# 19 of the 1024 tile dots: multiplied by GpSimd, summed by ScalarE

## The chip, the cores and the metric

The kernel runs on one core of one Trainium2 chip. The metric is the device time of one execution in microseconds (us), lower is better. The core has TensorE (PE in the profile; PEld is its weight load), VectorE (DVE), ScalarE (ACT), GpSimd (POOL) and SyncE (SP), which run their own instruction streams and meet at semaphores.

## What is computed

One inference step of a 2-layer hybrid recurrent decoder trunk, for 512 prompt tokens and 8 sample tokens, all in fp32. Layer 0 has a gated DeltaNet and a Mamba-2 mixer side by side, layer 1 a gated linear attention. Behind each mixer comes a retrieval over 16384 single-neuron experts, in which the change lies:

```python
def peer_ffn(h, w_q, keys1, keys2, u_tab, v_tab):
    def block(tb):
        q = (tb @ w_q).reshape(blk, PEER_HEADS, 2, half)
        ...
        v1, i1 = lax.top_k(s1, PEER_TOPK)
        v2, i2 = lax.top_k(s2, PEER_TOPK)
        cand = v1[..., :, None] + v2[..., None, :]
        ...
        top_s, top_j = lax.top_k(cand, PEER_TOPK)
        gate = jax.nn.softmax(top_s, axis=-1)
        pre = jnp.einsum('thkd,td->thk', u_tab[expert], tb)
        act = jax.nn.gelu(pre) * gate
        return jnp.einsum('thk,thkd->td', act, v_tab[expert])
```

Each token has 8 heads with 16 experts each, 128 picks. A pick reads one row of u (1024 numbers), which is multiplied with the token's vector and summed (the dot), and one row of v, which is weighed by gelu(dot) times the gate and added up.

## The kernel before

**Tiles and picks.** The prompt tokens make four tiles of 128, the sample tokens a fifth of 8. The kernel walks through `UNITS`, layer 0 tiles 0 to 3 and then layer 1 tiles 0 to 3, and in each unit through its 128 picks (8 sample picks are mixed into tile 3 of each layer): 1040 picks, numbered g from 0. For one pick, one gather brings the row [u, v] of 2048 numbers for each of 128 partitions, 1 MB, into slot g mod 8 of `ring`. Each half tile of 64 tokens is spread over the 128 partitions, so that picks 0 to 63 of a tile are its first half (w = 0) and picks 64 to 127 its second.

**One pick on each engine.** The order is fixed by hand, the same loop over g on every engine:
- GpSimd waits until `v_done` says that PE is done with pick g - 8, then issues the gather of g (L596).
- DVE waits for the gather and does the dot in one instruction, a product of `ring` and `htok` with a summed output into `pre` (L2357), and counts `dotted`.
- ACT waits for `dotted`, then runs three short operations: gelu into `act_v`, times the gate into `gated`, and a 128x64 scaled mask into `diag` (all recorded under the helper's line L1206).
- PE waits for `diag` and multiplies it with the v half of the ring slot (`tile_v`, two 128x512 products of a 64-column weight, recorded in four matmuls under the helper's line L613), and counts `v_done`.

**The work beside it.** Everything else of the model (projections, scans, norms, top-k choices of the next tiles) is written as generators, `front`, `choose` and `fold`, whose steps have slot numbers: behind pick g each engine runs all steps with a slot up to g. PE takes them two picks ahead (`LEAD`). So during picks 0 to 127 of tile 0 the second half of the even mixer runs: its input projection (two slots for a block of 8 matmuls), the copies of that projection out of PSUM on ACT, the convolution on DVE (L1637), the top-k choice for tile 1 on DVE (L2151 to L2179, with products over 128x2048 at L2100, L2104 and L2118, sums at L2106 and L2120, and the copies to `picked` and `gates` at L2126), and later the scan, with products on GpSimd too (L524). ACT has a table load (`ACT_TABLE_LOAD`) each time it goes from one kind of function to another that isn't in the loaded set.

**Queues.** Every engine works in order. GpSimd's queue holds the gathers, single DMAs for states and convolution rows, eight products of 264 columns (L507) and the products of the scan (L524). Weights are loaded by SP into `wring`.

## Time and profile before

| | us |
|---|---|
| median of 3 runs | 3359.38 (3356.14 to 3359.39) |
| the profiled execution | 3360.97, its span 3359.0 |
| busy PE, DVE, POOL, ACT | 2711.8, 2104.4, 1241.5, 1231.8 |
| 1024 tile dots on DVE (L2357) | 1243.2, 1227 ns each |
| mean granted TensorE clock | 0.84 |
| DMA moved | 1225.88 MB, mean 365 GB/s |

The page cuts the span into 40 slices of 84 us. In the slices from 588 us on, the DMA engines are busy for nine tenths nearly everywhere; in the fourth to seventh, from 252 to 588 us, it is 4, 6, 9 and 8 tenths, with 176 to 403 GB/s. How to read the views: the table of windows gives for each stretch of the span what each engine was busy, in us, and the TensorE clock granted; the rows in order of time give the start, the duration, the engine, the line, and in brackets the idle time before the instruction and what released it; the list of waits adds up such idle times by who waited for whom. Busy times of one engine can overlap a little, since an instruction may start while the one before it is draining.

### The profile page before, as it was taken

The numbers are of one execution on the slowest core, as the hardware profiler recorded it, in microseconds if no ns is written. First come the engines' busy times: TensorE is split into PE (matmuls) and PEld (weight loads), VectorE is DVE, ScalarE is ACT, GpSimd is POOL, SyncE is SP. The second block draws the span as 40 slices with busy tenths as digits, with TensorE's granted clock in tenths as the row PEclk, the third lists the DMA queues.
The fourth block names the chain that finished last, engine by engine and source line by source line (L and its number), as shares of the span: only waits on it lengthen the run. The fifth ranks groups of instructions, "written<-read, shape, count | busy, mean of one in ns | idle before, by whom it ended". The sixth has DMA issues, their size and how long they took to land.

```text
span 3359.0 us, 34624 instructions
## 1 busy us (share of the span) xinstructions
PE 2711.8 (81%) x11134; PEld 1371.6 (41%) x11134; DVE 2104.4 (63%) x4889; ACT 1231.8 (37%) x3752; POOL 1241.5 (37%) x1101
## 2 busy tenths in 40 slices
PE   8879997888988689788976789788789666676776
PEld 7767653444544145344522345344344111111132
DVE  4454688775656787576466785566546776744554
ACT  3211365442333343443333343532333343333332
POOL 0100133663433433344343433344333443433442
PEclk9889997996899789799988799797789776766677
DMA  4204698999999999999999999999899999999997
GB/s 158 76 1 176 246 403 329 389 395 375 408 408 395 401 419 395 388 388 387 418 421 421 405 419 409 368 390 413 368 412 372 400 419 421 397 422 422 421 419 327
DMA packets 186152, 1225.88 MB, mean 365 GB/s; under 512 B 21297, under 2 KB 24129, under 8 KB 50802
## 3 DMA queue, kind: packets, MB, share of 16 engines
q0 software_dynamic: 153024, 1115.00, 81.8%
q1 hardware_dynamic: 32946, 108.67, 8.6%
q8 instruction: 88, 1.44, 0.2%
q14 instruction: 94, 0.77, 0.1%
HBM read 1211.74 MB, written 11.84 MB: 364 GB/s over the span
## 4 chain that ended last, share of the span: by engine, by line
PE 48%; DMA 26%; DVE 15%; ACT 5%; issue 3%; DVEq 2%; POOL 1%; SPq 0%; ACTq 0%; POOLq 0%
PE ps L613 47%; DMA ring<-in_uv,picked 24%; DVE ring L2357 6%; DVEq L2149 1%; ACT scratch L1206 1%; ACT diag L1206 1%; ACT L1206 1%; DVE scratch L2100 1%; ACT gated L1206 1%; DMA scratch<-in_keys 1%; POOL ring L596 1%; ACT act_v L1206 1%; DVE scratch L2118 0%; DVE scratch L2104 0%; DVE ids L2106 0%
## 5 line engine op out<-in xcount | busy, mean ns | idle before, releaser
L596 POOL DMA_INDIRECT ring<-in_uv,picked x1024 | 1166.3, 1139 | 1744.6 <-PE ps L613 1635.3
L613 PE MATMUL ps<-ring,diag 128*64 128x512 f32 x4096 | 1339.8, 749 | 481.6 <-ACT diag L1206 474.7
L2357 DVE SCALAR_TENSOR_TENSOR ring<-ring,htok 128x1024 f32<-128x1024 f32 x1024 | 1243.2, 1227 | 596.0 <-DMA ring<-in_uv,picked 590.8
L613 PE MATMUL ps<-hT,wring 128*128 128x256 f32 (+1 forms) x3200 | 802.1, 401 | 18.4 <-DVE hT L1600 8.7
L1206 ACT ACTIVATE act_v<-pre 128x1 f32<-128x1 f32 x1040 | 209.5, 201 | 1467.3 <-DVE ring L2357 1466.3
L613 PEld LDWEIGHTS ps<-hT,wring 128*128 128x128 f32 x3200 | 602.6, 195 | 326.2 <-issue 229.8
L613 PEld LDWEIGHTS ps<-ring,diag 128*64 128x64 f32 x4096 | 245.1, 156 | 1188.4 <-ACT diag L1206 997.6
L1206 ACT ACTIVATE diag<-folded,gated 128x64 f32<-128x64 f32 x1024 | 356.2, 348 | 36.0 <-PE ps L613 2.7
L1206 ACT ACTIVATE gated<-act_v,gates 128x1 f32<-128x1 f32 x1024 | 301.7, 295 | 33.3
L613 PEld LDWEIGHTS ps<-scratch 128*128 128x128 f32 (+2 forms) x1428 | 201.5, 209 | 147.6 <-issue 85.5
L613 PE MATMUL ps<-scratch 128*128 128x128 f32 (+5 forms) x1428 | 238.0, 312 | 28.4 <-DVE scratch L1747 15.1
L1206 ACT ACTIVATE scratch<-ps 128x256 f32<-128x256 f32 (+5 forms) x118 | 64.7, 548 | 207.7 <-PE ps L613 206.9
L1206 ACT ACT_TABLE_LOAD x97 | 124.5, 1283 | 2.4 <-PEq L2463 0.7
L1206 ACT ACTIVATE keep<-ps 128x264 f32<-128x264 f32 (+4 forms) x147 | 43.6, 327 | 139.6 <-PE ps L613 139.5
L1637 DVE SCALAR_TENSOR_TENSOR keep<-keep,conv_w 128x256 f32<-128x256 f32 x120 | 58.1, 484 | 51.7 <-ACT keep L1206 43.1
L2357 DVE DVE_READ_ACCUMULATOR ring<-ring,htok 128x1 f32 x1024 | 83.5, 82 | 0.0
L524 POOL TENSOR_TENSOR scratch<-scratch,masks 128x512 f32<-128x512 f32 x18 | 25.9, 1447 | 152.1 <-DVE scratch L1724 141.0
L2306 DVE TENSOR_TENSOR xT<-xT,ps 128x512 f32<-128x512 f32 x15 | 10.3, 687 | 96.4 <-PE ps L1075 96.4
L2151 DVE MAX8 scratch<-scratch 128x8 f32<-128x128 f32 (+1 forms) x168 | 35.4, 259 | 56.1 <-ACT scratch L1206 55.4
L613 PE MATMUL ps<-gated,ring 128*128 128x1 f32 x256 | 42.6, 296 | 16.4 <-ACT gated L1206 16.4
L1620 DVE TENSOR_TENSOR xT<-ps,xT 128x256 f32<-128x256 f32 (+1 forms) x32 | 13.7, 428 | 64.9 <-PE ps L613 64.9
L613 PEld LDWEIGHTS ps<-gated,ring 128*128 128x128 f32 x256 | 41.3, 253 | 30.5 <-ACT gated L1206 30.5
(340 smaller groups left out, 1734.3 us busy)
## 6 DMA issues: line engine op xcount, KB each, us to landing
wring<-in_weights SPq DMA_DIRECT2D x200, 512.0 KB, 7.8
ring<-in_uv,picked POOLq DMA_INDIRECT x1024, 13.3
scratch<-in_keys POOLq DMA_DIRECT2D x4, 1024.0 KB, 14.6
scratch<-in_s_gla POOLq DMA_DIRECT2D x4, 1024.0 KB, 12.7
out_o_gla<-scratch POOLq DMA_DIRECT2D x4, 1024.0 KB, 12.8
scratch<-in_s_dn POOLq DMA_DIRECT2D x1, 2048.0 KB, 14.4
scratch<-in_s_ssm POOLq DMA_DIRECT2D x1, 2048.0 KB, 19.9
out_o_dn<-scratch POOLq DMA_DIRECT2D x1, 2048.0 KB, 11.8
```

The source lines that it names most:

```text
L524: pool.tensor_tensor(nl[:, (6 * m + l - 1) % 4, :].rearrange("p (h i) -> p h i", h=4), nmat, mask4(LEVEL0 + l), ALU.mult).then_inc(sem(f"n ...
L596: pool.indirect_dma_start(out=ring[:, g % RING, :], out_offset=None, in_=io["uv"][L], in_offset=bass.IndirectOffsetOnAxis(ap=index, axis=0 ...
L613: return pe.matmul(out, lhsT, rhs, start=start, stop=stop)
L1206: return act.activation(out, in_, func, **k)
L1620: tt(x, ps[:, 2 + b % 2, 0:n], x, ADD).then_inc(sem("gemm_free"), 1)
L1637: last = stt(y, x[:, 3 - s:259 - s], conv_w[:, j, 3 - s:4 - s], y, MUL, ADD)
L2100: tt(e, posf[R, H].rearrange("p h (k a) -> p (h k) a", a=1).to_broadcast(full), each(iota[:, :] if step == 8 else row_at).to_broadcast(ful ...
L2149: dve.drain()
L2151: dve.max(vals[:, 0:8], src)
L2306: last = tt(x, x, ps[:, w % 2, :].rearrange("p (c h i) -> p h c i", c=4, h=2), ADD)
L2357: stt(x, x, 1.0, h, MUL, MUL, accum_out=pre[:, g % SMALL:g % SMALL + 1]).then_inc(sem("dotted"), 1)
```

## The change

For picks 8, 11, ..., 62 of the first unit (`BY_POOL`, 19 picks) the dot is split. GpSimd multiplies the u half of the ring slot with `htok` in place, and ACT sums the product by a copy onto itself with an accumulated output into `pre`, in front of its three short operations. The instruction on DVE goes, and `dots(g)` turns a pick number into the number of dots that DVE has done by then. GpSimd's product for pick m stands in its queue right behind the gather of pick m + 5 (`MULTIPLY_LAG`). Besides, some semaphores are merged (`sample_ready` for three, `htok_mm` takes over `last_rows_mm`), with the same waits. The core of the diff:

```diff
+MULTIPLY_LAG = 5
+BY_POOL = list(range(8, HALF, 3))
+
+
+def dots(g):
+    return g - sum(m < g for m in BY_POOL)
...
@@ gpsimd, behind the gather of pick g @@
+                    m = g - MULTIPLY_LAG
+                    if m in BY_POOL:
+                        pool.wait_ge(sem(f"uv_loaded{m % RING}"), 16 * (m // RING + 1))
+                        pool.wait_ge(sem("fold_ready"), 1)
+                        pool.tensor_tensor(ring[:, m % RING, 0:D], ring[:, m % RING, 0:D], htok[:, 1, :], ALU.mult)\
+                            .then_inc(sem("multiplied"), 1)
                     front.upto(g)
...
@@ scalar, at pick g @@
-                    act.wait_ge(sem("dotted"), g + 1)
+                    if g in BY_POOL:
+                        n = BY_POOL.index(g) + 1
+                        act.wait_ge(sem("multiplied"), n)
+                        x = ring[:, g % RING, 0:D]
+                        f(x, x, ACT.Copy, accum_out=pre[:, s:s + 1]).then_inc(sem("summed"), 1)
+                        act.wait_ge(sem("summed"), n)
+                    else:
+                        act.wait_ge(sem("dotted"), dots(g + 1))
                     f(act_v[:, s:s + 1], pre[:, s:s + 1], ACT.Gelu_apprx_tanh).then_inc(sem("gelu_done"), 1)
...
@@ vector, at pick g @@
-                    dve.wait_ge(sem(f"uv_loaded{g % RING}"), 16 * (g // RING + 1))
                     x = ring[:, g % RING, 0:D]
                     if t == S:
                         x = x.rearrange("p (b i) -> p b i", b=2)
-                    stt(x, x, 1.0, h, MUL, MUL, accum_out=pre[:, g % SMALL:g % SMALL + 1]).then_inc(sem("dotted"), 1)
+                    if g not in BY_POOL:
+                        dve.wait_ge(sem(f"uv_loaded{g % RING}"), 16 * (g // RING + 1))
+                        stt(x, x, 1.0, h, MUL, MUL, accum_out=pre[:, g % SMALL:g % SMALL + 1]).then_inc(sem("dotted"), 1)
```

How the queues read at three places of the changed picks. First GpSimd from gather 41 on, before (gathers are the DMAs into `ring`):

```order
L596 DMA ring<-in_uv,picked 128x2048 x12
L514 DMA out_o_conv_s<-scratch 128x480
L515 DMA out_o_conv_p<-keep 128x60
L596 DMA ring<-in_uv,picked 128x2048 x14
L524 TENSOR_TENSOR scratch<-scratch,masks 128x512
```

and the same place now, from the product for pick 44 on:

```order
L611 TENSOR_TENSOR ring<-ring,htok 128x1024
L604 DMA ring<-in_uv,picked 128x2048 x3
L611 TENSOR_TENSOR ring<-ring,htok 128x1024
L522 DMA out_o_conv_s<-scratch 128x480
L523 DMA out_o_conv_p<-keep 128x60
L604 DMA ring<-in_uv,picked 128x2048 x3
L611 TENSOR_TENSOR ring<-ring,htok 128x1024
L604 DMA ring<-in_uv,picked 128x2048 x3
L611 TENSOR_TENSOR ring<-ring,htok 128x1024
```

The third product there is that for pick 50, behind gather 55; those for picks 53, 56 and 59 follow in the same rhythm, and that for pick 62 stands between the first two products of the scan (L532, before L524).

DVE in the choice for tile 1, before, from the dot of pick 47 to the dot of pick 49:

```order
L2357 SCALAR_TENSOR_TENSOR ring,pre<-ring,htok 128x1024
L2106 TENSOR_REDUCE ids<-scratch 128x128
L2108 CAST scratch<-ids 128x128
L2110 TENSOR_SCALAR scratch<-scratch 128x128
L2357 SCALAR_TENSOR_TENSOR ring,pre<-ring,htok 128x1024
L2112 CAST scratch<-scratch 128x128
L2115 SCALAR_TENSOR_TENSOR ids<-scratch,ids 128x128
L2116 TENSOR_TENSOR scratch<-scratch 128x128
L2100 TENSOR_TENSOR scratch<-scratch,pack 128x2048
L2357 SCALAR_TENSOR_TENSOR ring,pre<-ring,htok 128x1024
```

and now, with the product in front of it:

```order
L2125 TENSOR_TENSOR scratch<-scratch 128x2048
L2127 TENSOR_REDUCE ids<-scratch 128x128
L2129 CAST scratch<-ids 128x128
L2131 TENSOR_SCALAR scratch<-scratch 128x128
L2379 SCALAR_TENSOR_TENSOR ring,pre<-ring,htok 128x1024
L2133 CAST scratch<-scratch 128x128
L2136 SCALAR_TENSOR_TENSOR ids<-scratch,ids 128x128
L2137 TENSOR_TENSOR scratch<-scratch 128x128
L2121 TENSOR_TENSOR scratch<-scratch,pack 128x2048
L2379 SCALAR_TENSOR_TENSOR ring,pre<-ring,htok 128x1024
```

The dot between the second product over 2048 elements and its sum is gone.

ACT at picks 22 and 23, behind a table load; before there are six short operations between two table loads' groups, now a sum over 1024 columns stands in their middle:

```order
L1220 ACT_TABLE_LOAD
L1220 ACTIVATE act_v<-pre 128x1
L1220 ACTIVATE gated<-act_v,gates 128x1
L1220 ACTIVATE diag<-folded,gated 128x64
L1220 ACTIVATE ring,pre<-ring 128x1024
L1220 ACTIVATE act_v<-pre 128x1
L1220 ACTIVATE gated<-act_v,gates 128x1
L1220 ACTIVATE diag<-folded,gated 128x64
```

Only the row `ring,pre<-ring` is new there.

## Rows read from the trace of the kernel before

**Rows 1.** The chain that ended last, shares of the span by engine.
```profile
PE 48%; DMA 26%; DVE 15%; ACT 5%; issue 3%; DVEq 2%; POOL 1%; SPq 0%; ACTq 0%; POOLq 0%
```

**Rows 2.** Windows: stretch, length, busy us of each engine, PEclk, DMA, GB/s.
```profile
480.00:500.00 20.00, 20.00 (x84) 10.12 (x83) 18.50 (x58) 14.37 (x34) 5.82 (x7) 1.00 1.02 415
...
540.00:560.00 20.00, 10.77 (x48) 4.38 (x48) 19.13 (x20) 7.84 (x18) 6.12 (x5) 0.62 0.87 321
```

**Rows 3.** Waits from 400 to 528 us: total us, times, longest.
```profile
POOL ring L596 <- PE ps L613: 87.0, 39, 5.7
```

**Rows 4.** DVE in order of time: start, us, what; idle before in brackets.
```profile
567.84 0.19 DVE L1659 RECIPROCAL keep<-keep 8x8 f32<-8x8 f32 x1 [1.50 <-ACT keep L1206]
...
576.24 1.76 DVE L1715 TENSOR_TENSOR scratch<-scratch,masks 128x1536 f32<-128x1536 f32 x1 [1.25 <-ACT scratch L1206]
```

**Rows 5.** GpSimd and DVE in order of time, where both work.
```profile
354.44 5.66 POOL L507 TENSOR_TENSOR hT<-hT,otok 128x264 f32<-128x264 f32 x8 [22.58 <-ACT hT L1206]
...
592.12 1.21 DVE L2357 SCALAR_TENSOR_TENSOR ring<-ring,htok 128x1024 f32<-128x1024 f32 x1
593.03 1.43 POOL L524 TENSOR_TENSOR scratch<-scratch,masks 128x512 f32<-128x512 f32 x1
593.27 2.27 DVE L2357 SCALAR_TENSOR_TENSOR ring<-ring,htok 128x1024 f32<-128x1024 f32 x1
...
604.96 1.28 POOL L524 TENSOR_TENSOR scratch<-scratch,masks 128x512 f32<-128x512 f32 x1
605.44 0.68 DVE L1747 TENSOR_TENSOR scratch<-scratch,ps 128x512 f32<-128x512 f32 x1
```

**Rows 6.** The gathers (L596) of 440 to 520 us, issue to landing.
```profile
DMA to landing us min/median/max: 7.7/10.1/12.0
```

**Rows 7.** GpSimd's gathers 52 to 67 and DVE behind them, in order of time.
```profile
534.28 0.94 POOL L596 DMA_INDIRECT ring<-in_uv,picked  x1 [0.30 <-issue]
535.36 0.33 DVE L1648 TENSOR_TENSOR scratch<-scratch,conv_w 128x160 f32<-128x160 f32 x1
...
548.65 1.42 POOL L596 DMA_INDIRECT ring<-in_uv,picked  x1 [2.64 <-PE ps L613]
550.24 2.29 DVE L2100 TENSOR_TENSOR scratch<-scratch,pack 128x2048 f32<-128x2048 f32 x1
...
562.28 0.93 POOL L596 DMA_INDIRECT ring<-in_uv,picked  x1 [5.07 <-PE ps L613]
562.99 0.85 DVE L2126 COPY gates<-ids 64x64 f32<-64x64 f32 x4
...
572.29 0.96 DVE L1711 TENSOR_SCALAR scratch<-scratch 128x1536 f32<-128x1536 f32 x1
...
583.72 1.21 POOL L596 DMA_INDIRECT ring<-in_uv,picked  x1 [2.21 <-PE ps L613]
...
589.52 1.77 POOL L596 DMA_INDIRECT ring<-in_uv,picked  x1 [0.16 <-issue]
```

**Rows 8.** ACT, PE and GpSimd in order of time, around ACT's table loads.
```profile
449.31 1.40 POOL L596 DMA_INDIRECT ring<-in_uv,picked  x1 [2.05 <-PE ps L613]
...
455.55 1.28 ACT L1206 ACT_TABLE_LOAD   x1
...
462.12 0.35 ACT L1206 ACTIVATE diag<-folded,gated 128x64 f32<-128x64 f32 x1
462.88 0.65 PE L613 MATMUL ps<-ring,diag 128*64 128x512 f32 x2
...
465.38 1.06 ACT L1206 ACTIVATE keep<-keep 128x1024 f32<-128x1024 f32 x1
...
468.31 0.35 ACT L1206 ACTIVATE diag<-folded,gated 128x64 f32<-128x64 f32 x1
468.85 0.65 PE L613 MATMUL ps<-ring,diag 128*64 128x512 f32 x2
...
573.28 1.58 ACT L1206 ACTIVATE scratch<-scratch 128x1536 f32<-128x1536 f32 x2 [0.35 <-DVE scratch L1711]
```

More of the change, by code:

```diff
@@ L851, in sample_even @@
                 pe.wait_ge(sem("even_group"), 5)
-                pe.wait_ge(sem("sm_diag_ready"), 1)
+                pe.wait_ge(sem("sample_ready"), 1)
                 mm(ps[:, 4, 0:192], ones[0:NS_TOK, :], sm_diag[0:NS_TOK, :, :].rearrange("p b c -> p (b c)"))\
@@ L877, in sample_even @@
                 last.then_inc(sem("sm_o_mm"), 1)
-                pe.wait_ge(sem("sm_xd_ready"), 1)
+                pe.wait_ge(sem("sample_ready"), 2)
                 for b in range(NS_TOK):
@@ L997, in sample_odd @@
                 pe.wait_ge(sem("odd_group"), 5)
-                pe.wait_ge(sem("sm_q_ready"), 1)
+                pe.wait_ge(sem("sample_ready"), 3)
                 for q in range(4):
@@ L1069, in last_rows @@
                                       xT[:, 4 * h + c, TILE_AT[3] + HALF:TILE_AT[3] + P], ident)
-                    last.then_inc(sem("last_rows_mm"), 1)
+                    last.then_inc(sem("htok_mm"), 1)
             def turn(w):
@@ L1110, in choice @@
                     if t == 1 and L:
-                        pe.wait_ge(sem("dotted"), SAMPLE_G[0][-1] + 1)
+                        pe.wait_ge(sem("dotted"), dots(SAMPLE_G[0][-1] + 1))
                     if t == S:
@@ L1149, in spread @@
                 if b >= 2:
-                    pe.wait_ge(sem("dotted"), SAMPLE_G[L][b - 2] + 1)
+                    pe.wait_ge(sem("dotted"), dots(SAMPLE_G[L][b - 2] + 1))
                 for c in range(KD):
@@ L1200, in _ @@
                 last = mm(ps[HALF * s:HALF * s + HALF, 4, 0:1], folded[:, :], row_sum[:, 0:1])
-            last.then_inc(sem("last_rows_mm"), 1)
+            last.then_inc(sem("htok_mm"), 1)
         @block.scalar
@@ L1483, in choice @@
                             for v in BEFORE[SAMPLE[L]]:
-                                act.wait_ge(sem("dotted"), v)
+                                act.wait_ge(sem("dotted"), dots(v))
                             last = f(h_s[:, :, :], hT[:, :, 256:264], ACT.Copy)
@@ L1498, in folds @@
                         act.wait_ge(sem("fold_mm"), 2 * w - 1 + h)
-                        act.wait_ge(sem("dotted"), SUB_FIRST[w - 1])
+                        act.wait_ge(sem("dotted"), dots(SUB_FIRST[w - 1]))
                         f(htok[:, 1 + w % 2, 512 * h:512 * h + 512], ps[:, w % 2, :], ACT.Copy).then_inc(sem("fold_ready"), 1)
@@ L1532, in _ @@
                     if g == ROWS_AT + 2:
-                        act.wait_ge(sem("last_rows_mm"), 1)
+                        act.wait_ge(sem("htok_mm"), max(ROW_TILE) + 1)
                         f(last_y, ps[:, 4, :], ACT.Copy).then_inc(sem("last_rows"), 1)
@@ L1539, in _ @@
             f(s_root, ps[:, 3, 0:NS_TOK], ACT.Sqrt, scale=1.0 / D, bias=eps[:, 0:1]).then_inc(sem("root_ready"), 1)
-            act.wait_ge(sem("last_rows_mm"), 2)
+            act.wait_ge(sem("htok_mm"), max(ROW_TILE) + 2)
             f(row_sum[:, 2:3], ps[:, 4, 0:1], ACT.Sqrt, scale=1.0 / D, bias=eps[:, 0:1]).then_inc(sem("root_ready"), 1)
@@ L1797, in sample_even @@
                    ident[0:NS_TOK, 0:NS_TOK].rearrange("p (b a) -> p b a", a=1).to_broadcast([NS_TOK, NS_TOK, 24]), MUL)\
-                    .then_inc(sem("sm_diag_ready"), 1)
+                    .then_inc(sem("sample_ready"), 1)
                 yield slot(2)
@@ L1805, in sample_even @@
                     last = tt(sm_xd[r], conv[r, 12:16, S_], sm_bc[r, :, 16 + half:24:2].rearrange("p b k -> p k b"), MUL)
-                last.then_inc(sem("sm_xd_ready"), 1)
+                last.then_inc(sem("sample_ready"), 1)
                 yield slot(6)
@@ L2003, in sample_odd @@
                 yield slot(0)
-                tsc(sm_q, oproj[:, 0:4, 256:264], scale, None, MUL).then_inc(sem("sm_q_ready"), 1)
+                tsc(sm_q, oproj[:, 0:4, 256:264], scale, None, MUL).then_inc(sem("sample_ready"), 1)
                 dve.wait_ge(sem("sm_exp"), 2)
```

## The prediction, made before the result

> **What bounds the kernel now.** I read the chain that ended last first, then the stretch in which the changed picks run, in three views: the table of 20 us windows, the list of waits from 400 to 528 us, and the rows of each engine in order of time. The whole span is a stream of 1040 picks in a fixed order, of which each takes one slot of an 8-deep ring, so time lost or won at one pick moves all later picks. The chain names PE for 48%, the gather for 26% and DVE for 15% [rows 1]. The 19 dots that the change takes off DVE are picks 8, 11, ..., 62; they run between 407 us (dot 8) and 591 us (dot 62) of 3359 us. What a dot is worth is decided there and nowhere else.
>
> That stretch has two parts. From pick 8 to about pick 44 (407 to 528 us) **PE leads**: it is busy for 20.00 of 20 us at 480 to 500 while DVE has 1.5 us free and ACT 5.6 [rows 2]. GpSimd's gathers wait for PE, 87.0 us in 39 waits, and it starts one gather per 2.99 us, the time of one pick on PE [rows 3]. From about pick 45 to pick 63 (528 to 592 us) **DVE leads**: 19.13 of 20 us busy at 540 to 560 while PE has 10.77 us and its granted clock is 0.62 [rows 2]; PE now waits for ACT's diag, and ACT for the dot.
>
> **What the change removes.** A dot costs 1.22 us, and the next instruction of DVE starts 1.14 to 1.15 us after it (dot 63 at 592.12, dot 64 at 593.27) [rows 5]. In the part that PE leads, 13 dots (8 to 44) leave: worth nothing there, since their diag is ready before PE takes it. In the part that DVE leads, six leave (47, 50, 53, 56, 59, 62), 6 x 1.14 = 6.8 us at most. Two of them are not on DVE's path: after dots 52 and 53 DVE sits 1.50 us until ACT has written what it inverts at 567.84, and after the place of dot 56 it sits 1.25 us until ACT releases the product at 576.24 [rows 4]. So 4 x 1.14 = **-4.6 us**.
>
> **What it adds on GpSimd.** A two-input product of 264 columns took 5.66 / 8 = 0.71 us there and one of 512 columns 1.28 us [rows 5]. That is (1.28 - 0.71) / 248 = 2.3 ns a column, so 1024 columns take 1.28 + 512 x 0.0023 = **2.5 us**. Such a product shuts out DVE. Dot 64 starts at 593.27, as dot 63 ends and while GpSimd is in its product of 593.03 to 594.46, and takes 2.27 us instead of 1.21: the 1.19 us that the two overlap, nearly all of it [rows 5]. Not everything is shut out: a sum whose second input is in PSUM took 0.68 us beside a GpSimd product at 604.96 [rows 5]. So an instruction of DVE with both inputs in SBUF waits until GpSimd has ended, and one with an input in PSUM doesn't; I take one with a single input to go free too. The Trainium skill ("SBUF — State Buffer", Who interferes with whom) states this as an exclusive lock on a shared pair of ports that the first to start holds for its whole instruction; by that rule, the rows agree, and it speaks against this change. It adds that copies of fp32 between SBUF tensors in DVE's two-port mode are shut out as well, which bears on one row of rows 7 (the copies of gates) and on nothing else in the sum. The skill's "GPSIMD Engine Reference" (Elementwise — side-by-side cycle accounting) gives 4497 ns for 2048 columns; by half of it, an estimate of 2.25 us, the next sum would be about 1 us smaller.
>
> Where each of the six products lands follows from the program's order: the product for pick m is queued on GpSimd right behind gather m + 5, which waits until PE is done with pick m - 3. Gathers landed 10.1 us after issue in the middle and 12.0 us at most [rows 6], and gather m is then five picks old, about 15 us, so the product waits for no data. What DVE loses, from [rows 7], where the gathers 52, 55, 58, 61, 64 and 67 are the GpSimd rows:
> - pick 47: free from 534.28 + 0.94 = 535.22, ends 537.7. DVE is in a run of two-input products of 160 columns; the next, at 535.36, waits: 2.3 us.
> - pick 50: free from 550.07, ends 552.6; the product of 2048 columns at 550.24 waits: 2.3 us.
> - pick 53: free from 563.21, ends 565.7; the copies of gates and dot 52 wait: 2.4 us.
> - pick 56: free from about 572.4, when DVE's one input operation of 1536 columns has started at 572.29; it ends before DVE's next two-input work at 576.24: 0.
> - pick 59: free from 584.93, ends 587.4; DVE has two sums with an input in PSUM until about 585.9 and then dot 60: 1.5 us.
> - pick 62: free from 591.3, just behind the start of dot 63, then dot 64 waits 2.5 us where it waited 1.06 already, and GpSimd's own product for the scan comes later: 1.9 us, my value between 1.4 and 2.5.
> The sum is **+10.4 us**. The bounds are 0 (all six beside work with one input) and 6 x 2.5 = 15 us. I take the value near the upper end because three quarters of DVE's time in this part is in instructions with two inputs in SBUF or in copies.
>
> **What it adds on ACT.** A pass over 128x1024 in SBUF took 1.06 us at 465.38 [rows 8]; the summing copy is priced by it, no row shows the accumulation itself, so 1.0 to 1.4 us. ACT has 14.37 of 20 us busy at 480 to 500 us [rows 2], so 19 x 1.06 = 20 us mostly lies beside other work. Two places have no room. One is pick 53, whose sum stands before ACT's work for the scan at 573.28: 1.06 less the 0.35 us that ACT sat there [rows 8], **+0.7 us**. The other is picks 20 to 24, around ACT's table loads. Gather 25 is issued at 449.31 and ends at 450.7, the product for pick 20 ends at 453.2, its sum at 454.3, its three short operations at 455.2, those of pick 21 at 457.1 (its dot, behind a convolution that waits for an ACT copy held up by pick 17's sum, is ready about 456.2) and the copies of the projection at 458.1, where the first table load began at 455.55: 2.5 us late. Then comes pick 22, whose diag started at 462.12 and ended at 462.47 when PE took it at 462.88 (0.4 us of slack), the sum for pick 23 (1.06 us more) and pick 24, whose diag ended at 468.66 for a PE that took it at 468.85 (0.2 us) [rows 8]. 2.5 + 1.1 - 0.2 = **+3.4 us**, and PE leads there, so the end pays it. Bounds: 0, if the product is early, and 5 us.
>
> In the rest of the part that PE leads, diag is 2 to 7 us ahead of PE, and a product costs this lead 2 to 4 us for the moment; I put it at 0.
>
> **Sum.** -4.6 + 10.4 + 0.7 + 3.4 = +9.9 us. The profiled execution took 3360.97 us (span 3359.0), so it would take 3370.9 us; it was 1.6 us above the median of 3359.38 us, so the median becomes **3369.3 us**. What a measurement of this kernel tells from no change is 0.2%, 6.7 us.
>
> **The rivals.**
> - *The port is cheap* (faster). If GpSimd gets its turn only when DVE is in an instruction with one input or waits for ACT, DVE loses nothing and keeps the relief of all six: 3359.4 - 6.8 = 3352.6 us. It decides below 1.14 us lost per product. For it: DVE has reduces of 2.29 us and sums from PSUM, and the 56 case. Against it: in [rows 5] GpSimd's product of 593.03 gets its turn as dot 63 ends, ahead of dot 64. Chance 0.14, of which 0.10 are faster by over 0.2%. The skill's page "Perfetto Trace Analysis" (Optimizing Scalar/DVE Operations) says that moving work off a saturated DVE may make sense and also that between these two engines it might not help; that is this rival and my forecast side by side.
> - *ACT has room*. The table loads hide in PE's lead and only the port is paid: 3359.4 + 6.5 = 3365.9 us. For it: its diag is 2 to 7 us ahead of PE at most picks. Chance 0.20, 0.12 of it within 0.2%.
> - *The product comes too late everywhere*. From PE's end of pick m - 3: gather 1.2, product 2.5, sum 1.1, three short operations 0.95, the copies 1.0, the convolution and top-k on DVE 2.3, dot m + 1 1.15, its three 0.95, which is 11.2 us for a PE that wants it after 10.9. With a port wait, each of 13 products then costs about 1 us: 3369.3 - 3.4 + 13 = 3378.9 us. Chance 0.15.
> - *Given back later*: after 600 us the gathers carry much of the path, and a shift at pick 63 is absorbed, 3359 to 3361 us. Against it: a gather waits for PE's pick eight back, so it moves along. Chance 0.13.
> - *It doesn't do what it says*: excluded, the order has 19 products on GpSimd, 19 sums on ACT and 19 dots fewer on DVE.
>
> **How the numbers follow.** The forecast itself has 0.38, of which 0.02 within 0.2%. Faster: 0.10. Same: 0.04 + 0.12 + 0.13 + 0.02 = 0.31. Slower: 0.36 + 0.08 + 0.15 = 0.59. The likeliest case gives 3369.3 us. Its own unknowns (port 5 to 15 us, ACT 0 to 5 us) make 3361 to 3376; the range reaches over most of the late product and of the absorbed case, 3355 to 3380 us, and leaves out the full relief.
>
> **What would show it.** Right: 19 products on GpSimd of 2.4 to 2.6 us; dots and 2048-column products of DVE with a share of 2 us and more longer than now; PE waiting for ACT's diag at picks 22 and 24; dot 64 starting about 10 us later. Wrong: no DVE instruction grown between 528 and 592 us (port), or pick 63 done no later than now.

## The result, and the profile after

The changed kernel takes **3386.37 us** (median of 4 runs, 3382.02 to 3387.32) where the kernel before took 3357.76 us beside it (4 runs, 3353.45 to 3359.39): a ratio of 1.0077, 95% interval 1.0064 to 1.0090. It is slower, as predicted, but by 28.6 us and not by 10, and that lies outside the range. The profiled execution spans 3385.5 us; the span was 3359.0 before.

The page of the changed kernel: busy time of each engine, the chain that ended last, and two groups of instructions.

```profile
PE 2713.2 (80%) x11134; PEld 1364.4 (40%) x11134; DVE 2125.2 (63%) x4851; ACT 1255.1 (37%) x3790; POOL 1275.2 (38%) x1120
...
PE 43%; DMA 26%; DVE 17%; ACT 7%; issue 3%; DVEq 2%; POOL 1%; another core or an unknown queue 0%; SPq 0%; POOLq 0%; ACTq 0%
...
L1658 DVE SCALAR_TENSOR_TENSOR keep<-keep,conv_w 128x256 f32<-128x256 f32 x120 | 73.9, 616 | 52.1 <-ACT keep L1220 44.1
```

DVE lost 19 dots and is still busy for **longer**: 2125.2 us against 2104.4. The convolution's products, which nobody touched, have a mean of 616 ns, and of 484 ns on the page before:

```profile
L1637 DVE SCALAR_TENSOR_TENSOR keep<-keep,conv_w 128x256 f32<-128x256 f32 x120 | 58.1, 484 | 51.7 <-ACT keep L1206 43.1
```

In the chain PE has gone from 48% to 43%, DVE from 15% to 17% and ACT from 5% to 7% [rows 1].

The windows of [rows 2] in the changed kernel, with the wait of [rows 3] (from 400 to 528 us) under them:

```profile
480.00:500.00 20.00, 20.00 (x83) 10.17 (x84) 18.08 (x51) 10.26 (x29) 10.26 (x8) 1.00 0.99 390
540.00:560.00 20.00, 7.89 (x16) 1.18 (x16) 17.63 (x43) 15.12 (x28) 9.90 (x9) 0.55 0.77 282
...
POOL ring L604 <- PE ps L627: 59.3, 27, 5.9
```

PE still has no free time at 480 to 500 us, but gathers wait for it only 27 times and not 39. At 540 to 560 us PE is down from 10.77 to 7.89 us. The windows are fixed in time: what stands in the second one now ran 10 to 15 us earlier before, so they show how full the engines are and not what one piece of work costs.

Where the time is lost is read from the gathers, since gather g starts when PE is done with pick g - 8. The gathers 10 and 76 of the kernel before:

```profile
400.63 0.94 POOL L596 DMA_INDIRECT ring<-in_uv,picked  x1 [2.94 <-PE ps L613]
...
613.80 1.38 POOL L596 DMA_INDIRECT ring<-in_uv,picked  x1 [1.57 <-PE ps L613]
```

and of the changed kernel:

```profile
398.23 0.94 POOL L604 DMA_INDIRECT ring<-in_uv,picked  x1 [2.93 <-PE ps L627]
...
641.15 1.39 POOL L604 DMA_INDIRECT ring<-in_uv,picked  x1 [1.56 <-PE ps L627]
```

The first is 2.40 us early, ahead of any product, which is only how one execution differs from another. The stretch between the two is 242.92 us long and was 213.17: **29.75 us** more. The span is 26.5 us longer from a start that is 2.4 us early, so 28.9 of it is still there at the end. I call this the shift of a kernel, and read it at two places: at pick 41 (gather 49), about where PE stops leading, and at pick 68 (gather 76). Up to pick 20 it is under 1 us. It grows by 6.7 us at picks 21 to 23, by 3.5 at 32 and 33, by 9.2 at 42 to 45 (2.0 of it gone at pick 46), by 7.7 at 52 to 54 (4.7 of it gone at pick 56), by 5.2 at 57 to 60 and by 3.4 at 61 and 62. A gather can also start late because GpSimd itself is late, so single picks stand out and fall back; what counts is what stays.

The product itself is as predicted, 19 of them at 2.35 to 2.52 us:

```profile
L611 POOL TENSOR_TENSOR ring<-ring,htok x19: 2349/2358/2515, 408.1 to 613.2; 128x1024 f32<-128x1024 f32 x19
```

What it does to DVE, in order of time (start, us, what; one pair around ScalarE's table loads, and three of the DVE-led part):

```profile
457.59 3.59 DVE L2379 SCALAR_TENSOR_TENSOR ring<-ring,htok 128x1024 f32<-128x1024 f32 x1
457.73 2.36 POOL L611 TENSOR_TENSOR ring<-ring,htok 128x1024 f32<-128x1024 f32 x1
...
538.50 2.35 POOL L611 TENSOR_TENSOR ring<-ring,htok 128x1024 f32<-128x1024 f32 x1
538.72 3.21 DVE L2379 SCALAR_TENSOR_TENSOR ring<-ring,htok 128x1024 f32<-128x1024 f32 x1
...
565.45 2.95 DVE L2136 SCALAR_TENSOR_TENSOR ids<-scratch,ids 128x128 f32<-128x128 f32 x1
565.88 2.37 POOL L611 TENSOR_TENSOR ring<-ring,htok 128x1024 f32<-128x1024 f32 x1
...
579.06 2.50 POOL L611 TENSOR_TENSOR ring<-ring,htok 128x1024 f32<-128x1024 f32 x1
579.46 2.76 DVE L2147 CAST picked<-ids 64x64 uint32<-64x64 f32 x4
```

A dot of 1.21 us takes 3.59 us, the whole product more, although its record starts 0.14 us before the product's. An operation of 128 columns takes 2.95 us. The product for pick 44 is the second pair: it stands at 538.50, five gathers behind its own, behind gather 49, which before was issued at 529.83, and so already in the part that DVE leads.

### The profile page after: what moved, and what is told of

Its sections match the earlier page's. It is cut to its first block, busy times and chain, and to the rows that moved or that the text cites. A ratio compares the mean times of both kernels' runs of the same rounds, so it can differ in the third digit from the quotient of the medians.

```text
span 3385.5 us, 34662 instructions
## 1 busy us (share of the span) xinstructions
PE 2713.2 (80%) x11134; PEld 1364.4 (40%) x11134; DVE 2125.2 (63%) x4851; ACT 1255.1 (37%) x3790; POOL 1275.2 (38%) x1120
## 3 DMA queue, kind: packets, MB, share of 16 engines
q8 instruction: 88, 1.44, 0.2%
## 4 chain that ended last, share of the span: by engine, by line
PE 43%; DMA 26%; DVE 17%; ACT 7%; issue 3%; DVEq 2%; POOL 1%; another core or an unknown queue 0%; SPq 0%; POOLq 0%; ACTq 0%
PE ps L627 43%; DMA ring<-in_uv,picked 24%; DVE ring L2379 6%; ACT L1220 1%; DVEq L2170 1%; ACT diag L1220 1%; ACT gated L1220 1%; ACT scratch L1220 1%; POOL ring L604 1%; DMA scratch<-in_keys 1%; DVE scratch L2121 1%; DVE keep L1658 1%; ACT act_v L1220 1%; ACT keep L1220 1%; DVE scratch L2125 0%
## 5 line engine op out<-in xcount | busy, mean ns | idle before, releaser
L604 POOL DMA_INDIRECT ring<-in_uv,picked x1024 | 1154.5, 1127 | 1740.0 <-PE ps L627 1634.6
L1658 DVE SCALAR_TENSOR_TENSOR keep<-keep,conv_w 128x256 f32<-128x256 f32 x120 | 73.9, 616 | 52.1 <-ACT keep L1220 44.1
L532 POOL TENSOR_TENSOR scratch<-scratch,masks 128x512 f32<-128x512 f32 x18 | 24.7, 1381 | 151.7 <-DVE scratch L1745 141.4
L627 PEld LDWEIGHTS ps<-masks,keep 128*128 128x128 f32 x288 | 39.4, 212 | 24.9 <-issue 24.8
## 6 DMA issues: line engine op xcount, KB each, us to landing
scratch<-in_s_gla POOLq DMA_DIRECT2D x4, 1024.0 KB, 12.5
scratch<-in_s_dn POOLq DMA_DIRECT2D x1, 2048.0 KB, 14.9
```

The source lines that it names most:

```text
L532: pool.tensor_tensor(nl[:, (6 * m + l - 1) % 4, :].rearrange("p (h i) -> p h i", h=4), nmat, mask4(LEVEL0 + l), ALU.mult).then_inc(sem(f"n ...
L604: pool.indirect_dma_start(out=ring[:, g % RING, :], out_offset=None, in_=io["uv"][L], in_offset=bass.IndirectOffsetOnAxis(ap=index, axis=0 ...
L627: return pe.matmul(out, lhsT, rhs, start=start, stop=stop)
L1658: last = stt(y, x[:, 3 - s:259 - s], conv_w[:, j, 3 - s:4 - s], y, MUL, ADD)
```

## The experiments

Each kernel's ratio is to the kernel before, run beside it. One execution differs from another by some us, so the ratio says how much and the shift, from one trace, says where; the two agree within 7.4 us (the most is e1, 16.1 us by the shift and 8.7 by the ratio). The two kernels e2 and e3 have a shift of 1.6 us at pick 41 although nothing that slows them lies before it, and e1 and the changed kernel, which run the same up to there, differ by 2.4 us, so that column is good to 2.4 us. The last column is how much longer than before (2104.4 us) DVE was busy.

| kernel | what runs | ratio, 95% interval | shift at pick 41 | at pick 68 | DVE busy |
|---|---|---|---|---|---|
| changed | all | 1.0077, 1.0064 to 1.0090 | 10.1 | 29.8 | +20.8 |
| e1 | picks 8 to 44 only | 1.0026, 1.0014 to 1.0037 | 12.5 | 16.1 | +15.6 |
| e2 | picks 47 to 62 only | 1.0031, 1.0019 to 1.0043 | 1.6 | 14.8 | +1.9 |
| e3 | 19 dots dropped | 0.9983, 0.9971 to 0.9994 | 1.6 | -1.7 | -20.1 |
| e4 | all dots, free product | 1.0071, 1.0044 to 1.0099 | 9.1 | 29.9 | +39.0 |
| e11 | the same, half as long | 1.0033, 1.0017 to 1.0049 | 2.3 | 16.3 | +27.2 |
| e8 | all dots, memset | 1.0045, 1.0030 to 1.0060 | 1.4 | 9.3 | +9.7 |
| e5 | all dots, free sum | 1.0031, 1.0021 to 1.0042 | 2.0 | 7.6 | +1.3 |
| e7 | changed without sums | 1.0076, 1.0056 to 1.0097 | 8.1 | 22.2 | +14.9 |
| e6 | product after 3 gathers | 1.0041, 1.0026 to 1.0057 | 10.1 | 20.1 | +13.5 |
| e12 | e6 without sums | 1.0038, 1.0023 to 1.0053 | 9.2 | 15.8 | +14.8 |
| e15 | e12 without 17, 20, 23, 26 | 1.0019, 1.0008 to 1.0031 | 0.5 | 7.8 | +9.5 |
| e13 | e6, signal after 5 | 1.0043, 1.0025 to 1.0061 | 6.9 | 20.6 | +17.3 |
| e14 | e3, signal after 5 | 0.9986, 0.9975 to 0.9998 | 0.6 | -2.6 | -18.5 |
| e9 | changed without 17, 20, 23 | 1.0060, 1.0042 to 1.0078 | 9.5 | 26.6 | +15.6 |
| e10 | changed without 59, 62 | 1.0057, 1.0040 to 1.0073 | 10.1 | 23.4 | +21.8 |

**The two halves of the picks.**

```diff
-BY_POOL = list(range(8, HALF, 3))
+BY_POOL = list(range(8, 45, 3))       # e1
+BY_POOL = list(range(47, HALF, 3))    # e2
```

> The change for picks 8 to 44 alone (13 products), the stretch where PE led before. In the profile of the changed kernel the gathers are +12 us behind the kernel before at pick 41 to 44, counted from their lead of 2.4 us before the first product. If the two stretches add up, this kernel is 10 to 13 us slower than before. My recorded sum had 3.4 us for it; if the loss here is later hidden under DVE's work from pick 45 on, it is under 5 us.

> The change for picks 47 to 62 alone (6 products), the stretch where DVE led. My recorded sum had +6.5 us. If the stretches add up as the profile of the changed kernel has it, +14 to +18 us. If what was lost there came from engines that were already out of step from the first stretch, under 8 us.

The shifts add up: 16.1 + 14.8 = 30.9 us, against 29.8. The ratios give 0.26% + 0.31% = 0.57% against 0.77%, which their intervals just allow. By the shifts, the 13 picks that I had priced at 3.4 us cost as much as the six that I had priced at 6.5.

**The relief alone.** e3 takes the products and the sums out and lets ACT wait for the gather, so the dots of 19 picks are left out.

```diff
-                        act.wait_ge(sem("multiplied"), n)
-                        x = ring[:, g % RING, 0:D]
-                        f(x, x, ACT.Copy, accum_out=pre[:, s:s + 1]).then_inc(sem("summed"), 1)
-                        act.wait_ge(sem("summed"), n)
+                        act.wait_ge(sem(f"uv_loaded{g % RING}"), 16 * (g // RING + 1))
```

> The 19 dots are left out altogether: no product on GpSimd, no sum on ACT, ACT uses an old number in their place and waits for the gather alone. This is the most that taking them off DVE can give. By my count 6 dots lie in the stretch where DVE leads and 4 of them on its path: 4.6 to 6.8 us faster than before. If DVE's load reaches PE in the first stretch too, more: up to 19 x 1.14 = 22 us.

Nothing is won up to pick 41, 3.3 us from there to pick 68 (1.6 to -1.7). So 19 dots for nothing are worth 0.17%, and the six that count are worth about three. The merged semaphores of the change are in e3 too, and its shift is 0.0 us up to pick 38: they cost nothing.

**The product alone.** In e4 all dots stay on DVE, and GpSimd's product has another output and is waited for by nobody; e11 halves it, and e8 puts a memset of the same length as e11's product in its place.

```diff
+                        pool.tensor_tensor(otok[:, D // 2:D].bitcast(mybir.dt.bfloat16), htok[:, 1, :], htok[:, 1, :], ALU.mult)           # e4
+                        pool.tensor_tensor(otok[:, D // 2:D // 2 + 256].bitcast(mybir.dt.bfloat16), htok[:, 1, 0:512], htok[:, 1, 0:512], ALU.mult)   # e11
+                        pool.memset(otok[:, D // 2:D].bitcast(mybir.dt.bfloat16), 0.0)           # e8
```

> All dots stay on DVE; GpSimd does 19 products of 1024 columns at the same places of its queue, on htok alone, into a buffer that nobody reads. No sum on ACT and nobody waits for the product. Theory port (a product keeps DVE out of its two-input instructions for its whole length): 19 x 2.4 us of DVE time lost and no dot saved, so at least as slow as the changed kernel, 28 to 40 us slower than before. Theory queue (the time is lost because ACT waits in order for product and sum): under 12 us slower.

> As the kernel with the product alone, but GpSimd fills the unused buffer with zeros instead of multiplying (it writes and reads nothing in SBUF). Shows whether GpSimd's use of SBUF for reads is what keeps DVE out. Theory port, reads: DVE's instructions keep their lengths and the kernel is within 3 us of before. If any GpSimd instruction on SBUF shuts DVE out, it is slower by its own length each time.

> The kernel with all dots on VectorE and a product on GpSimd that nobody waits for, now over 512 columns instead of 1024, some 0.95 us long, as long as the memset of the run before (0.97 us, the kernel 14 us slower by its median, the stage 8.7 us longer). If the port is what costs, VectorE's busy time grows by nearly the whole of each product (19 x 0.9 = 17 us, against 9.7 us with the memset), and the stage by about half of what the full product gave (29 us): 14 to 18 us, the kernel at 3368 to 3375 us. If it is the place in GpSimd's queue that costs, this run gives what the memset gave, a stage 8 to 9 us longer and VectorE's busy time up by 10 us at most.

The lines of GpSimd's operation in e4, e11 and e8 (min, median, max in ns):

```profile
L613 POOL TENSOR_TENSOR otok<-htok x19: 1899/1900/1911, 408.2 to 615.1; 128x1024 bf16<-128x1024 f32 x19
...
L613 POOL TENSOR_TENSOR otok<-htok x19: 1046/1047/1048, 411.6 to 604.8; 128x512 bf16<-128x512 f32 x19
...
L613 POOL MEMSET otok<- x19: 965/965/970, 410.7 to 599.1; 128x1024 bf16 x19
```

e4 has a shift as large as the changed kernel's with no wait for GpSimd in it: ScalarE waits for DVE's dots there and for no product. So the product alone can cost that much. That the two figures are equal is chance, since e4 keeps its 19 dots, has shorter products and no sums. Half the length gives half the shift, 16.3 us. The memset, of nearly the same length and in the same places of the queue, gives 9.3, and DVE is busy for 9.7 us more, where e11 has 27.2. So the inputs that GpSimd reads cost VectorE's time, on top of what a memset does. (The ratios of e8 and e11, 1.0045 and 1.0033, don't tell the two apart; the shift and DVE's busy time do.) A dot and a small copy of DVE in e8, each with its memset:

```profile
420.08 1.21 DVE L2374 SCALAR_TENSOR_TENSOR ring<-ring,htok 128x1024 f32<-128x1024 f32 x1
420.17 0.96 POOL L613 MEMSET otok<- 128x1024 bf16 x1
...
478.51 1.70 DVE L1649 COPY keep<-keep 128x3 f32<-128x3 f32 x1
479.22 0.96 POOL L613 MEMSET otok<- 128x1024 bf16 x1
```

The dot goes on beside the memset in its usual 1.21 us; the copy takes 1.70 us, where such a copy has 0.17. The memset is therefore not free for DVE either. Of the 9.7 us, 8.3 lie in six places, all of them copies, casts or an operation with a constant (TENSOR_SCALAR), each with one input tensor, in SBUF; no dot beside a memset took more than 1.22 us. How much of the 9.3 us of shift is that and how much the gathers behind the memset in the queue stays open. The Trainium skill ("SBUF — State Buffer", Who interferes with whom) has both: a DVE instruction with two SBUF inputs contends with GpSimd instructions that read and not with those that only write, and, without that distinction, copies, casts and the like in the two-port mode contend with GpSimd.

**The sum alone.** e5 adds 19 summing copies to the kernel before, of `htok`, into a spare output; e7 takes them out of the changed kernel (the sums of 19 picks are left out, ACT only waits for the product).

```diff
+                        f(otok[:, D // 2:D].bitcast(mybir.dt.bfloat16), htok[:, 1, :], ACT.Copy, accum_out=spare_sum[:, 0:1]).then_inc(sem("summed"), 1)   # e5
...
-                        f(x, x, ACT.Copy, accum_out=pre[:, s:s + 1]).then_inc(sem("summed"), 1)   # e7
```

> All dots stay on DVE, nothing on GpSimd; ACT does 19 summing copies over 1024 columns (of htok, their result unused) in front of its three short operations at the same picks. It prices ACT's part by itself. My recorded sum had 1.06 us each, of which 0.7 + about 1 us reach the end: 1 to 4 us slower. Theory queue: ACT's load is what counts, 8 us or more.

> The changed kernel without the sum: product on GpSimd and no dot on DVE for the 19 picks, ACT waits for the product but does not sum it (an old number is used). The difference to the changed kernel is the price of the 19 sums in place. Theory port: 1 to 6 us faster than the changed kernel. Theory queue: 8 us or more faster.

Both give 7.6 us of shift, 2.0 of it up to pick 41 (where I had put 3.4) and the rest behind it (0.7). A sum is two instructions, here at pick 62 of the changed kernel:

```profile
615.72 1.06 ACT L1220 ACTIVATE ring<-ring 128x1024 f32<-128x1024 f32 x1 [5.64 <-POOL ring L611]
616.69 0.19 ACT L1220 ACTIVATION_READ_ACCUMULATOR ring<-ring 128x1 f32 x1
```

The ratios of the changed kernel and of e7, though, hardly differ (1.0077 and 1.0076, intervals of 0.2%), so the sum's price is known to some 7 us only.

**Is the product too late?** e6 moves it up to three gathers behind its own, and e12 takes e6's sums out as well (left out for 19 picks).

```diff
-MULTIPLY_LAG = 5
+MULTIPLY_LAG = 3
```

> The changed kernel with the product behind the gather of pick m + 3 instead of m + 5, so some 6 us earlier. Theory queue (ACT waits for a product that comes late): much of the 28 us comes back, the kernel is under 15 us slower than before. Theory port: each product shuts out DVE all the same, 23 us or more slower than before.

> The changed kernel with the product three gathers behind its own instead of five, and without ScalarE's sum (ScalarE only waits for the product; the sums of the 19 picks are left out). With three gathers nobody waited for a product, so this leaves the relief (stage 1.7 us shorter when alone) and what the product does to VectorE. If lateness (about 10 us of stage between five and three gathers) and the sum (about 8 us) add up, the stage is 10 to 14 us longer than before and the kernel at 3363 to 3368 us. If they overlap (the sum costs only because the product is late), it stays near the run with three gathers, 18 to 20 us of stage, 3370 to 3375 us.

In e6 9.7 us of the shift are back, all behind pick 41, and no engine waits for a product any more; the changed kernel had this:

```profile
ACT act_v L1220 <- DVE ring L2379: 74.4, 24, 7.1
ACT ring L1220 <- POOL ring L611: 20.4, 6, 5.6
```

That looks like lateness, and I took it for that. e13 tests it: the products stay where e6 has them, and only ScalarE's signal comes from a one-column memset where the changed kernel's product stood. e14 is e3 with that signal (no products and sums).

```diff
+                    m = g - 5                                             # e13, behind the product of g - 3
+                    if m in BY_POOL:
+                        pool.wait_ge(sem("multiplied"), 2 * BY_POOL.index(m) + 1)
+                        pool.memset(mark[:, 0:1], 0.0).then_inc(sem("multiplied"), 1)
...
-                        act.wait_ge(sem("multiplied"), n)
+                        act.wait_ge(sem("multiplied"), 2 * n)
```

> The kernel with the product three gathers behind its own, but ScalarE waits for a one-column memset of GpSimd that stands where the product stood in the changed kernel, five gathers behind. The products fall where they fall with three gathers (stage 20.1 us longer than before, nobody waits for a product). If lateness makes the 9.7 us between that and the changed kernel (29.8), the stage is 26 to 30 us longer here, the kernel at 3378 to 3386 us. If it is the place of the products, it stays at 19 to 22 us and the kernel at 3366 to 3374 us.

> The 19 dots dropped, no product and no sum, and ScalarE waits at those picks for the row and for a one-column memset that GpSimd does five gathers behind (the products and sums of these 19 picks are left out). If being late costs by itself, the stage is 4 to 9 us longer than before, nearly all of it behind pick 44, the kernel some 3 to 8 us over before. If lateness costs only together with what the products take from VectorE, the stage stays near the run with the dots dropped, 1.7 us shorter than before, within 2 us.

The theory falls. e13 keeps e6's shift (20.6 against 20.1), and e14 is as fast as e3; ScalarE does wait for the mark there, 13.3 us in 7 times, and it costs nothing. So a signal five gathers late is not the price. What differs between e6 and the changed kernel is what the products fall on, and that the product's own 2.4 us come on top of the late place. By the gathers, the changed kernel is behind e6 by 1.9 us at pick 48, 4.4 at 50, 6.5 at 56, 8.9 at 57 and 9.7 at 62. The last of these places can be read, in the next paragraph; what makes the others stays open.

**The end of the stretch.** e10 leaves out the picks 59 and 62 of the changed kernel.

```diff
-BY_POOL = list(range(8, HALF, 3))
+BY_POOL = list(range(8, 57, 3))
```

> The changed kernel without the picks 59 and 62 (17 products). If what the last part costs is that ScalarE waits for products that stand late in GpSimd's queue (5.6 us at pick 62, handed on to VectorE's wait of 10.8 us for TensorE), the stage ends 6 to 9 us earlier than in the changed kernel and the kernel takes 3377 to 3381 us. If VectorE's time lost under the products 47 to 56 makes it (they hold instructions of the top-k choice), under 3 us come back and it stays at 3383 to 3387 us.

6.3 us of the shift are back. Pick 62 in the changed kernel, GpSimd, ACT, PE and DVE in order of time:

```profile
609.97 1.28 POOL scratch L532
611.40 1.77 POOL ring L604
613.19 2.51 POOL ring L611
615.72 1.16 ACT ring L1220 x2
...
617.72 0.58 ACT L1220 ACTIVATE scratch<-ps 128x512 f32<-128x512 f32 x1
618.35 2.08 PE L627 MATMUL ps<-scratch 128*128 128x128 f32 x8 [3.00 <-ACT scratch L1220]
624.30 0.69 DVE L1766 TENSOR_TENSOR scratch<-scratch,ps 128x512 f32<-128x512 f32 x1 [10.81 <-PE ps L627]
```

(The first four lines are from the chain, with their start and time.) The product stands behind gather 67 and GpSimd's own scan product before it. It holds nothing of DVE, which waits for PE by then, so no port is in it. ScalarE waits 5.64 us for the product, and behind the sum in its queue stands the copy that the scan on PE needs; PE waits for that copy, DVE for PE. Here it is the wait for the product.

**ScalarE's table loads.** e9 leaves out the picks 17, 20 and 23 of the changed kernel. e15 leaves 17, 20, 23 and 26 out of e12 (their dots are back on DVE, the other 15 picks stay without a sum).

```diff
+BY_POOL = [m for m in range(8, HALF, 3) if m not in (17, 20, 23)]       # e9
+BY_POOL = [m for m in range(8, HALF, 3) if m not in (17, 20, 23, 26)]   # e15
```

> The changed kernel without the picks 17, 20 and 23 (their dots go back to VectorE, 16 products are left). In the trace of the changed kernel the end of pick 23 on TensorE is 7.5 us later than before, counted from the end of pick 10, and none of it had come by pick 18. If the table loads of ScalarE there (picks 20 to 24) were stretched by its sums, as I predicted, or by products that hold the dots of VectorE, the shift at pick 25 falls to under 2 us and the kernel to 3375 to 3380 us. If VectorE has spare time around there and catches up in either case (rival: the shift is made by other products of the part, and moves to the next table load), the shift comes a few picks later and the kernel stays at 3382 to 3387 us.

> The run with three gathers and no sum, with the dots of picks 17, 20, 23 and 26 back on VectorE (the other 15 picks are still left unsummed). With all 19 products the end of pick 25 on TensorE was 8.6 us late and VectorE had been held by products at 434, 444, 453 and 463 us, ahead of ScalarE's two rows of table loads. If only products ahead of table loads cost in the part that TensorE leads, the shift at pick 40 falls from 9.2 us to under 3 us (1.6 of it stands in runs that change nothing there), and the stage from 15.8 to 8 to 10 us. If the next products do the same to what follows, the shift at pick 40 stays above 5 us.

e9 halves the shift at pick 25 (7.5 to 3.7 us), less than the fall to under 2 us that I had expected. Its trace shows the rest: the product for pick 14, at 433.59, also stands ahead of the table loads. The three convolution products at 432.91 take 4.44 us with it instead of 1.61, the four table loads start 2.5 us late, and PE waits 2.05 us for the diag of pick 22. e15 is clear: at pick 41 the shift is 0.5 us instead of 9.2. Nine other products up to there cost nothing. How four of them cost so much is read in e12, GpSimd and DVE, then ACT and PE in order of time:

```profile
443.51 3.89 DVE L2376 SCALAR_TENSOR_TENSOR ring<-ring,htok 128x1024 f32<-128x1024 f32 x1
443.95 2.36 POOL L611 TENSOR_TENSOR ring<-ring,htok 128x1024 f32<-128x1024 f32 x1
...
453.20 2.36 POOL L611 TENSOR_TENSOR ring<-ring,htok 128x1024 f32<-128x1024 f32 x1
454.15 1.44 DVE L1651 COPY keep<-keep 128x3 f32<-128x3 f32 x1 [0.99 <-ACT keep L1220]
...
458.00 1.22 DVE L2376 SCALAR_TENSOR_TENSOR ring<-ring,htok 128x1024 f32<-128x1024 f32 x1
```

and behind that:

```profile
459.26 0.20 ACT L1220 ACTIVATE act_v<-pre 128x1 f32<-128x1 f32 x1 [4.34 <-DVE ring L2376]
...
460.99 1.28 ACT L1220 ACT_TABLE_LOAD   x1
...
465.70 1.28 ACT L1220 ACT_TABLE_LOAD   x1
...
467.56 0.35 ACT L1220 ACTIVATE diag<-folded,gated 128x64 f32<-128x64 f32 x1
...
467.96 1.98 PE L627 MATMUL ps<-ring,diag 128*64 128x512 f32 x4 [4.68 <-ACT diag L1220]
```

The dot at 458.00, that of pick 21, is itself not held, but it is late: before, it stood at 452.56. Three products in a row, those for picks 17, 20 and 23, have held DVE: the one at 434.50 a dot (3.93 us), the one at 443.95 another (3.89 us), the one at 453.20 a copy of three columns in front of this dot (1.44 us instead of 0.17). ScalarE waits 4.34 us for it, where it waited 2.97 us before:

```profile
453.82 0.20 ACT L1206 ACTIVATE act_v<-pre 128x1 f32<-128x1 f32 x1 [2.97 <-DVE ring L2357]
```

The four table loads stand behind that dot's operations in a fixed order, so they start at 460.99 where they started at 455.55 [rows 8], the next diag comes at 467.56 instead of 462.12, and PE stops for 4.68 us. The lead over PE was enough for the table loads, and not for them and the products ahead of them.

## Why the prediction came out as it did

Right were the direction and the mechanism: GpSimd's product shuts out DVE's instructions with two inputs in SBUF for its whole length (e4: 39.0 us of DVE for 19 products of 1.90 us). So were the product's time (2.5 us predicted, 2.36 measured), the sum's 1.06 us, the products of picks 47 and 50 (2.3 us of DVE each; the instructions at 548.57 and 565.45 took 2.92 and 2.95 us, of which the operation itself is 0.3), pick 56 beside nothing, pick 53 (the casts at 579.46 took 2.76 us instead of 0.80; 2.4 us predicted), and PE waiting for the diag of pick 22 (4.29 us), though not for that of pick 24.

Not right was that an instruction with a single input goes free. It holds for DVE's searches and reduces (in e6 the reduce of 2048 columns at 571.88 keeps its 2.29 us beside the product of 570.25 to 574.03). It doesn't hold for copies and casts, which I had excepted at pick 53, nor for operations with a constant, which I had not. In e4:

```profile
592.10 2.84 DVE L1727 TENSOR_SCALAR scratch<-scratch 128x1536 f32<-128x1536 f32 x1
592.21 1.90 POOL L613 TENSOR_TENSOR otok<-htok 128x1024 bf16<-128x1024 f32 x1
```

That is the instruction of 0.96 us beside which I had put the product for pick 56 at 0. In the changed kernel this product runs from 593.60 to 595.95, while DVE waits for ScalarE; that it cost nothing was luck.

Its size was wrong, and two steps failed, both of them costs that I had put at 0: what the products do to DVE in the part that PE leads, and the place of the products five gathers behind. The terms, with what the shifts give for them:

- **Relief**, -4.6 predicted: -1.7 in all, -3.3 behind pick 41 (e3), which is what three dots are worth and not four.
- **Port**, +10.4: e12 has relief and port alone, 15.8, so the port is 15.8 + 1.7 = **17.5 us**. Behind pick 41 it is 6.6 + 3.3 = 9.9, near my term, though in the places of e12 and not in those that I had worked out. The other 7.6 us are in the part that PE leads, and there I had written "I put it at 0". This is the first step that failed. I had set the lead of 2 to 7 us against one product of 2.4, where several add up, and had looked at the table loads only for ScalarE's sums and the late products (3.4 us) and not for DVE, though my own step noted 0.4 and 0.2 us of slack there. With the sums gone from e12, the jump is all there; with four products gone, none is.
- **Which products lie in which part.** I went by the picks, six of them behind 528 us. The product of pick 44 stands behind gather 49, which was issued at 529.83 before, and so belongs to the part that DVE leads, which I priced without it. e1, which has no later product, still goes from 12.5 to 16.1 us behind pick 41. (The changed kernel grows by 9.2 us between picks 41 and 45, but the product for pick 47 has a share in that.)
- **Single places**: pick 59 held DVE for 0.4 us (1.5 predicted, the dot at 605.82 took 1.57), and yet at that pick the changed kernel is 2.6 us behind e10, which lacks this product; pick 62 held it for nothing (1.9), but made ScalarE wait.
- **The sum**, 0.7 + 3.4 = 4.1: 20.1 - 15.8 = 4.3 with three gathers (e6, e12), 7.6 with five.
- **Lateness**, 0: five gathers instead of three are worth 9.7 us. This is the second step that failed, and the largest single miss. "The product waits for no data" was true and not the question; what the product stands behind and what stands behind it was. For pick 62 the cause is shown, for the rest of the 9.7 us it is open.

-1.7 + 17.5 + 4.3 + 9.7 = 29.8 us, the shift of the changed kernel (the differences are taken one behind the other, so they have to add up; single traces make each of them uncertain by 1 to 2 us). In another order the terms come out otherwise: with the sums gone the lateness is 22.2 - 15.8 = 6.4 us (e7, e12), and e7, which lacks the 19 dots and has longer products than e4, has 7.7 us less shift than e4, so beside the products the dots seem to be worth more than the 1.7 us of e3.

The rival of the product that comes too late everywhere gave 3378.9 us, the nearest figure, but not for its reason: ScalarE waited for 6 of 19 products, and e13 and e14 show that the late signal alone costs nothing. The cheap port and the room on ScalarE are out by e4 and e5. Of the shift 0.9 us was given back later (29.8 to 28.9), so that rival is out too.

## To carry to other kernels

An engine that is not the bound still has a lead that is spent once: look for the places where its consumer has a long fixed block in its queue (here four table loads), and subtract there everything that the change adds, on each engine of the chain, not only on the one that it touches. Moving work from VectorE to GpSimd pays only if what GpSimd does leaves VectorE alone; here each product took from VectorE about twice what the dot had cost. And when work is queued some steps behind its own item, sort it into the stages of the kernel by when it runs, not by the item's number.

## What the hardware showed beside that

- **The one whose record starts first isn't always the one that goes on.** DVE's dots and products that started up to 0.5 us before the product were held for its whole length (457.59 against 457.73; 565.45 against 565.88). The second of these takes 0.29 us by itself and would have been over before the product's record starts. In e8 the copy at 478.51 was held although the memset's record starts 0.71 us behind it. Dots that started 0.9 us before it kept their 1.22 us, and the product took 2.50 us. The Trainium skill ("SBUF — State Buffer", Who interferes with whom) has it that whoever issues first gets the ports; these rows agree only if the start of a record isn't taken for the issue, which can mislead by up to 0.7 us. For long instructions the exclusion works both ways. In e6 a product waits for a running instruction of DVE and the next one of DVE, 2.29 us by itself, waits for the product:

```profile
554.26 2.30 DVE L2121 TENSOR_TENSOR scratch<-scratch,pack 128x2048 f32<-128x2048 f32 x1
555.24 3.53 POOL L611 TENSOR_TENSOR ring<-ring,htok 128x1024 f32<-128x1024 f32 x1
556.64 4.28 DVE L2125 TENSOR_TENSOR scratch<-scratch 128x2048 f32<-128x2048 f32 x1
```

- **A sum with an input in PSUM goes free.** Beside the product at 603.79 three of them took their usual 0.68 us, the first of them here, and the dot behind them waited:

```profile
603.79 2.52 POOL L611 TENSOR_TENSOR ring<-ring,htok 128x1024 f32<-128x1024 f32 x1
604.02 0.68 DVE L1752 TENSOR_TENSOR scratch<-ps,scratch 128x512 f32<-128x512 f32 x1
...
605.82 1.57 DVE L2379 SCALAR_TENSOR_TENSOR ring<-ring,htok 128x1024 f32<-128x1024 f32 x1
```

- **A short product takes more than its length.** With 19 products of 1.05 us DVE was busy for 27.2 us longer, 1.4 us each: an instruction that starts just before the product is held from its own start (a dot at 432.61 took 2.45 us instead of 1.21 beside a product of 1.05 us at 432.92).
